# Sample values in the areas of the transposed input, the recurrence on head tiles, and an output stage that begins in halves

## The reference

```
h = rms_norm(x) @ w_in          # 8720 columns: q, k, v of 3 x 8 heads, az, gq, gk, gv, gz, glr, gates mg_a, mg_b
o_attn = softmax-weighted sum over three groups of windowed attention: (window 128, dilation 1), (512, 4), (2048, 16)
         sample tokens attend to cached k, v rows and to their own new rows
o_gla  = gated linear recurrence, 4 heads, key 64, value 128, state S:
         o = (q e^b)(k e^-b)^T masked @ v + (q e^b) @ S ;  S' = e^b_last * S + (k e^(b_last-b))^T @ v
mixed  = sigmoid(mg_a) * ((o_attn * silu(az)) @ w_attn_out) + sigmoid(mg_b) * ((rms_norm(o_gla) * silu(gz)) @ w_gla_out)
y      = rms_norm(x + mixed @ w_out)
```

## Time and profile before

| | |
|---|---|
| Median of three runs | 2516.12 us |
| The profiled execution, its own time | 2519.2 us |
| Its span, first to last instruction | 2517.4 us |
| TensorE busy | 2462.3 us, 98% of the span |
| VectorE, ScalarE, GpSimd busy | 1216.4, 907.9, 197.1 us |
| DMA moved | 416.97 MB, mean 166 GB/s |
| Chain that ended last | TensorE 93%, DMA 3%, VectorE 2% |
| Mean granted TensorE clock | 0.992 of full |

### The profile page before, as it was taken

One profiled execution on the slowest core, in us unless ns is written; L12 is line 12 of the kernel. 1 busy time (PEld: TensorE's weight loads), 2 busy tenths in 40 slices (PEclk: granted clock), 3 DMA queues, 4 the chain that ended last, 5 costly groups with the idle time before them and its releaser, 6 DMA issues.

```text
span 2517.4 us, 36888 instructions
## 1 busy us (share of the span) xinstructions
PE 2462.3 (98%) x13660; PEld 1976.9 (79%) x13660; DVE 1216.4 (48%) x2858; ACT 907.9 (36%) x2161; POOL 197.1 (8%) x360
## 2 busy tenths in 40 slices
PE   9999999999999999999999999999999977999998
PEld 6888887887778888887888888787777634888887
DVE  5323423243321125565665666557665346655663
ACT  5224534443432224224545544555243322212221
POOL 0000000000000000121111111222222100000000
PEclk9999999999999999999999999999999988999999
DMA  5333333232333224467777656887776598343431
GB/s 191 103 121 112 104 110 116 89 99 91 119 106 99 90 78 141 141 193 232 219 220 222 208 180 208 258 255 229 209 223 206 193 322 314 149 159 139 160 153 67
DMA packets 204929, 416.97 MB, mean 166 GB/s; under 512 B 32160, under 2 KB 46000, under 8 KB 202640
## 3 DMA queue, kind: packets, MB, share of 16 engines
q1 hardware_dynamic: 163360, 295.69, 35.3%
q0 software_dynamic: 29072, 92.96, 12.8%
q10 hardware_dynamic: 12320, 25.96, 2.7%
HBM read 313.33 MB, written 112.99 MB: 169 GB/s over the span
## 4 chain that ended last, share of the span: by engine, by line
PE 93%; DMA 3%; DVE 2%; SPq 1%; ACT 1%; issue 1%; POOL 0%; DVEq 0%; ACTq 0%
PE b_acc L1229 20%; PE b_acc L1231 19%; PE b_acc L1230 19%; PE c_p_s L1279 3%; PE c_p_o L1302 3%; PE c_p_t L1290 3%; PE c_p_qk L1266 3%; PE f_p_b L1894 2%; PE f_p_b L1896 2%; PE f_p_b L1895 2%; PE f_p_z L1894 2%; PE f_p_z L1896 2%; PE f_p_z L1895 2%; PE b_acc L1235 2%; PE b_acc L1236 1%; PE e_p_o L1824 1%
## 5 line engine op out<-in xcount | busy, mean ns | idle before, releaser
L1229 PE MATMUL b_acc<-b_whi,hT_hi 128*128 128x512 f32 x2048 | 819.5, 400 | 3.7 <-DVE b_wlo L965 1.5
L1231 PE MATMUL b_acc<-b_whi,hT_lo 128*128 128x512 f32 x2048 | 799.0, 390 | 0.0
L1230 PE MATMUL b_acc<-b_wlo,hT_hi 128*128 128x512 f32 x2048 | 798.3, 390 | 0.0
L1229 PEld LDWEIGHTS b_acc<-b_whi,hT_hi 128*128 128x128 f32 x2048 | 384.4, 188 | 100.9 <-issue 9.4
L1231 PEld LDWEIGHTS b_acc<-b_whi,hT_lo 128*128 128x128 f32 x2048 | 384.4, 188 | 82.5
L1230 PEld LDWEIGHTS b_acc<-b_wlo,hT_hi 128*128 128x128 f32 x2048 | 385.0, 188 | 73.3
L965 DVE SCALAR_TENSOR_TENSOR b_wlo<-b_raw,a_lnw,b_whi 128x512 fp32r<-128x512 f32 x268 | 192.8, 749 | 362.2 <-ACT b_whi L757 361.8
L771 ACT COPY b_stage<-b_acc 128x512 f32<-128x512 f32 (+2 forms) x198 | 115.3, 583 | 539.6 <-PE b_acc L1231 529.4
L795 ACT ACTIVATE c_sm<-c_sm,c_ends 128x256 f32<-128x256 f32 (+1 forms) x384 | 172.8, 451 | 129.7 <-DVE c_ends L1050 129.6
L757 ACT ACTIVATE b_whi<-b_raw,a_lnw 128x512 fp32r<-128x512 f32 x268 | 182.8, 714 | 3.8 <-ACT c_og L813 1.4
L769 ACT ACTIVATE b_stage<-b_acc 128x512 f32<-128x512 f32 x96 | 57.4, 598 | 308.4 <-PE b_acc L1231 308.2
(11 more groups left out here) (308 smaller groups left out, 3104.1 us busy)
## 6 DMA issues: line engine op xcount, KB each, us to landing
b_raw<-in_w_in SPq DMA_DIRECT2D x134, 512.0 KB, 4.4
tm<-b_stage SPq DMA_DIRECT2D x256, 256.0 KB, 2.1
a_x<-tm POOLq DMA_DIRECT2D x192, 256.0 KB, 5.0
b_ck<-in_cache_kv_w POOLq DMA_DIRECT2D x104, 256.0 KB, 5.2
c_qk<-tm SPq DMA_DIRECT2D x101, 256.0 KB, 3.7
f_m<-tm SPq DMA_DIRECT2D x16, 1024.0 KB, 5.8
c_v<-tm SPq DMA_DIRECT2D x53, 256.0 KB, 4.0
og<-c_og ACTq DMA_DIRECT2D x48, 264.0 KB, 4.1
```

The costliest lines, as they stand in the source:

```text
L1229: nc.tensor.matmul(out, stat_hi, mov_hi, start=(k == 0), stop=False)
L1230: nc.tensor.matmul(out, stat_hi, mov_lo, start=False, stop=False)
L1231: return nc.tensor.matmul(out, stat_lo, mov_hi, start=False, stop=(k == KC - 1))
```

## The change

- The value tiles 5 to 12 (`HV`) are loaded into the areas of `hT_hi` and `hT_lo`: token tile t of the second half gives its place to value tile 5 + t when the last slot that reads it is done. A tile lies there in four units, two in each of the two areas, a unit as four pieces of 128 columns with a stride of 1024, and is loaded by four DMAs (two for the half tile). SP issues them in the loop of the projection, in the last eight slots. Tiles 18 to 20 (`HV_AGAIN`) go to the places of tiles 5 to 7 once these are used. The rest pass through the ring of five.
- The recurrence's states are loaded without zeros, 128 x 128 a pair of heads and sequence; `gla_out` does two products of 64 rows by 128 columns where it did one of 128 x 256, `gla_outer(j)` does two sequences in eight products of 64 x 64 by 128; there are four `gla_outer` instead of eight. The clearing of the state on GpSimd goes.
- The branch weights have four raw buffers (`w_raw2` lies in the room that the smaller state leaves). All eight splits come after tile 20 has been used. SP's order of loads is written out anew.
- The output stage begins in another order: half of branch product 1, the mixed transposes of tile 0, the other half; VectorE's `mix(0)` is taken apart in `weigh` and `add`, and the output weights are split around them. The first two output weights are loaded as soon as all value tiles are used.

The diff, cut to its core:

```diff
+                    if s > NSLOT - TPH:
+                        late_tile(s - (NSLOT - TPH) - 1)
...
+HV = range(VSLOTS, VSLOTS + TPH)
+HV_AGAIN = range(18, 21)
...
+        v_h = [h_sb("e_v_hT_hi", [P, KC, HTOK]), h_sb("e_v_hT_lo", [P, KC, HTOK])]
...
-            G["state"] = sb("g_state", [P, DB, NP, 2 * GV_W])
+            E = dict(vc=[sb("e_vc_whi", [P, 4, CH])], v_h=v_h)
+            E["w_raw2"] = sb("w_raw2", [P, 2, D])
+            G["state"] = sb("g_state", [P, DB, NP, GV_W])
...
-    p_go = g_bank[1][0:NS, :]
-    p_u = [g_bank[2], g_bank[0]]
+    p_go = [g_bank[1][0:NS, 0:NP * GV_W], g_bank[2][0:NS, 0:NP * GV_W]]
+    p_u = [g_bank[k][:, :].rearrange("p (j a e) -> p j a e", j=2, a=NP) for k in (0, 2)]
...
+    in_h = lambda w: w in HV or w in HV_AGAIN
+    ring = [w for w in range(V_PER_PAIR * NPAIR) if not in_h(w)]
+    h_tile = lambda w: w - (HV_AGAIN.start if w in HV_AGAIN else HV.start)
+    h_loads = lambda w: 32 if w % V_PER_PAIR == 0 else 64
+
     def vc(w):
-        return vc_a[:, w % VSLOTS, :, :] if w % VSLOTS < 2 else vc_b[w % VSLOTS - 2]
+        k = ring.index(w) % VSLOTS
+        return vc_a[:, k, :, :] if k < 2 else vc_b[k - 2]
+
+    def v_cols(w, u):
+
+        if not in_h(w):
+            return vc(w)[:, u, :]
+        t = h_tile(w)
+        return v_h[u // 2][:, 4 * (u % 2):4 * (u % 2) + 4, t * P:(t + 1) * P]
...
+            if w in HV:
+                sp.wait_ge(over.mm_done, over.products - TPH + h_tile(w) + 1)
+            elif w in HV_AGAIN:
+                sp.wait_ge(v_used, HV[h_tile(w)] + 1)
+            elif ring.index(w) >= VSLOTS:
+                sp.wait_ge(v_used, ring[ring.index(w) - VSLOTS] + 1)
...
+            if in_h(w):
+                t = h_tile(w)
+                for u in range(2 if r == 0 else 4):
+                    sp.dma_start(v_cols(w, u), src[:, u, :].rearrange("l (x e) -> l x e", x=4)).then_inc(v_h_in[t // 4], 16)
+                return
...
-            wb_after = (6, 7, 9, 10, 14, 15, 18, 20)
-            for w in range(VSLOTS, V_PER_PAIR * NPAIR):
...
+            for k in range(STAGES):
+                sp.wait_ge(over.stored[k], over.stores[k])
+            sp.wait_ge(over.scored, over.scores)
+            load_vn(1)
+            sp.dma_start(diag[:, :], A["dec_diag"]).then_inc(gw_in, 16)
+            sp.dma_start(gw[:, :], A["gla_norm_w"].rearrange("a (p b) -> p (a b)", b=1)).then_inc(gw_in, 16)
+            sp.dma_start(g_v[:, :], TMs[SEQ:TOK, TM_GV * CH:(TM_GV + 1) * CH]).then_inc(g_st_in, 16)
+            load_v(13)
+            load_v(14)
+            for h in range(GH):
+                r = slice(GK * (h % 2), GK * (h % 2) + GK)
+                sp.dma_start(g_state[r, :, h // 2, :], A["state_gla"][0, :, h, :, :].rearrange("b k v -> k b v")
+                             ).then_inc(g_st_in, 16)
+            for w in (15, 16, 17):
                 load_v(w)
...
-            sp.wait_ge(v_used, 24)
+            for i in range(4):
+                load_wb(i)
+            for w in HV_AGAIN:
+                load_v(w)
+            load_vn(2)
+            branches_free(sp)
+            load_branches(0)
+            load_gates(0)
+            load_v(21)
+            load_vn(3)
+            sp.wait_ge(g_o_evacd, 1)
+            sp.dma_start(OL[SEQ:TOK, :], g_out[:, :]).then_inc(g_stored, 16)
+            for w in range(22, 26):
+                load_v(w)
+            load_branches(1)
+            load_wb(4)
+            load_v(26)
+            load_wb(5)
+            load_v(27)
+            load_wb(6)
+            load_wb(7)
+            sp.wait_ge(w_lo, 2 * G4)
+            load_m(0)
+            sp.wait_ge(v_used, 25)
...
+            sp.wait_ge(v_used, V_PER_PAIR * NPAIR)
+            load_wo(0)
+            load_wo(1)
             load_branches(2)
             load_gates(2)
             gla_over(sp)
             sample_over(sp)
-            wo = A["w_out"].rearrange("a (c p) e -> p (a c) e", p=P)
-            for c in range(KC):
-                if c >= 4:
-                    sp.wait_ge(w_lo, 2 * G4 + c - 3)
-                sp.dma_start(wo_raw[c % 4], wo[:, c, :]).then_inc(wo_in[c % 4], 16)
-                if c == 3:
-                    load_m(0)
+            for c in range(2, KC):
+                load_wo(c)
...
-                    nc.tensor.matmul(p_go[:, 2 * GV_W * a:2 * GV_W * (a + 1)], g_qm[:, a, NS * j:NS * j + NS],
-                                     g_state[:, j, a, :], start=(a == 0 and j == 0), stop=False)
-            for h in range(GH):
-                cols = slice(GV_W * h, GV_W * (h + 1))
-                last = nc.tensor.matmul(p_go[:, cols], g_att[:, h % 2, h // 2, :], g_v[:, cols], start=False,
-                                        stop=(h == GH - 1))
+                    for h in range(2):
+                        r = slice(GK * h, GK * h + GK)
+                        last = nc.tensor.matmul(p_go[h][:, GV_W * a:GV_W * (a + 1)], g_qm[r, a, NS * j:NS * j + NS],
+                                                g_state[r, j, a, :], start=(a == 0 and j == 0), stop=False)
+            last.then_inc(g_o_done, 1)
...
+            if j == 1:
+                pe.wait_ge(g_o_evacd, 1)
             if j >= 2:
-                pe.wait_ge(g_u_read, NP * (j - 1))
-            for a in range(NP):
-                cols = slice(2 * GV_W * a, 2 * GV_W * (a + 1))
-                last = nc.tensor.matmul(p_u[j % 2][:, cols], g_km[:, a, j, :], g_v[:, cols], start=True, stop=True)
+                pe.wait_ge(g_u_read, 2 * NP * (j - 1))
+            for i in range(2):
+                for h in range(GH):
+                    a, r = h // 2, slice(GK * (h % 2), GK * (h % 2) + GK)
+                    last = nc.tensor.matmul(p_u[j % 2][r, i, a, :], g_km[:, a, 2 * j + i, r], g_v[:, GV_W * h:GV_W * (h + 1)],
+                                            start=True, stop=True)
...
-                pe.wait_ge(w_lo, 2 * G4)
+                pe.wait_ge(w_lo, G4)
                 pe.wait_ge(outed, 2 * NPAIR - 3)
-            for a in range(2):
+            for a in parts:
                 if t == 0 and a == 1:
+                    pe.wait_ge(w_lo, 2 * G4)
...
-            gla_outer(1)
             pv_new(2)
             pv(2, 0, 0)
             pv(2, 1, 0)
+            gla_outer(1)
+            pv(2, 2, 0)
+            turn_p(3)
             gla_outer(2)
+            pv(2, 2, 1)
             gla_outer(3)
-            turn_p(3)
-            pv(2, 2, 0)
-            gla_outer(4)
-            gla_outer(5)
-            pv(2, 2, 1)
-            gla_outer(6)
-            gla_outer(7)
             pv_new(3)
             pv(3, 0, 0)
             pv(3, 1, 0)
             pv(3, 2, 0)
             transpose_branches(0)
             pv(3, 2, 1)
-            for t in range(TILES):
+            branch_products(0)
+            transpose_branches(1)
+            keep_running(12)
+            branch_products(1, (0,))
+            transpose_mixed(0)
+            branch_products(1, (1,))
+            out_products(0, 0)
+            transpose_branches(2)
+            out_products(0, CH)
+            transpose_mixed(1)
+            for t in range(2, TILES):
...
+            act.wait_ge(raw_in[i % 4], 16 * (i // 4) + 16)
+            act.wait_ge(v_used, HV_AGAIN.stop)
...
+            scale_ol(0)
+            for i in range(2 * G4):
+                split_wb_hi(i)
...
         def mix(t):
+            weigh(t)
+            add(t)
+
+        def weigh(t):
...
+            output(2)
+            for i in range(G4):
+                split_wb_lo(i)
             gla_advance(3)
-            split_wb_lo(5)
-            gla_advance(4)
-            gla_advance(5)
-            output(2)
-            gla_advance(6)
-            gla_advance(7)
-            gn_steps()
-            split_wb_lo(6)
-            split_wb_lo(7)
-            branches(0)
+            for i in range(G4, 2 * G4):
+                split_wb_lo(i)
             split_lo1(0)
             output(3)
             branches(1)
-            for c in range(4):
+            split_wo_lo(0)
+            split_wo_lo(1)
+            weigh(0)
+            split_lo1(1)
+            add(0)
+            for c in range(2, 6):
                 split_wo_lo(c)
-            for t in range(TILES):
+            split_lo2(0)
+            for c in range(6, KC):
+                split_wo_lo(c)
+            branches(2)
+            for t in range(1, TILES):
```

More of the change, by code:

```diff
@@ L1466, in plan_late @@
 def plan_late(nc):
+    over_h, h_sb, _, _ = scope(nc)
+    with over_h:
+        v_h = [h_sb("e_v_hT_hi", [P, KC, HTOK]), h_sb("e_v_hT_lo", [P, KC, HTOK])]
     held, h_sb, _, _ = scope(nc)
@@ L1571, in finish @@
     mask_in, lse_in, gw_in = sem("e_mask_in"), sem("e_lse_in"), sem("w_gw_in")
-    raw_in = [sem("w_raw_in0"), sem("w_raw_in1")]
+    v_h_in = [sem("e_v_hT_in0"), sem("e_v_hT_in1")]
+    raw_in = [sem(f"w_raw_in{k}") for k in range(4)]
     w_hi, w_lo = sem("w_hi"), sem("w_lo")
@@ L1702, in tail, with tile @@
                 load_v(q + 1)
+        def tile(t):
```

(15 more changed lines are left out.)

165 lines of the change are left out of this document (71 added, 94 removed).

## The result

The changed kernel, called after in this text, takes 2503.32 us (median of 5 runs, 2502.86 to 2504.80), the kernel before in the same comparison 2518.88 us (5 runs, 2514.57 to 2519.72): the ratio is 0.9945, 95% interval 0.9930 to 0.9959. It is 15.6 us faster. The profiled execution of after takes 2504.8 us, 14.4 less than that of before. The forecast of 2490 us promised 25.7 us between the profiled executions; 2503 lies inside the range of 2475 to 2504, but the gain is little more than half of what was forecast.

A forecast was written before the change was run, and what follows sets the result against it. The sample stage was taken as bound by the bytes behind its value tiles, with half-idle DMA engines just ahead. 2519.2 - 18.7 - 7.0 = 2493.5 us profiled; the median shown is 3.1 lower, so 2490, range 2475 to 2504.

The forecast's parts named there:

- Gain 36.8 - 29.0 - 0.8 = 7.0 us: First branch product to first output product: 29.0 us instead of 36.8, 0.8 for transposes moved later; bounds -9.4 and -3.
- new wait of 2.4 us: Output stage, ahead of the first half of branch product 1: TensorE waits 2.4 us in place of 6.6.
- The sample stage: Projection end to first branch product: early head tiles bring that product 18.7 us earlier, ends 11.1 and 26.4.
- The price of the pieces: Head tiles loaded in 512 B pieces: 270 GB/s, 3.9 us a tile, with ends 4.8 and 3.0 us.
- TensorE loses nothing to this before 1999.4: End of the projection: loading head tiles there costs TensorE 0 us, since a slot's store is wanted about 23 us later.
- both new waits: Sample stage: TensorE waits 6.1 us at the recurrence's small inputs and 6.3 us at the new values of pair 2.
- no waits for the value tiles of pairs 0 and 1: Sample stage, sign in the profile after: TensorE no longer waits for these value tiles.
- the recurrence products: Recurrence on head tiles: 64 records take 3.5 us, where 16 products took 7.07 us before.
- the first (full rate): Rival on head tile loads: 512 B pieces go at 392 GB/s like large ones, giving 2481 us; chance 0.13.
- the third (a price from 7 us a tile upwards): Rival: costly pieces make head tiles fill the queue far into the sample stage, 2533 us at 125 GB/s; chance 0.05.
- The second: Rival: small pieces go at 217 GB/s and output weights come late, gain 11.1 + 3, 2502 us; chance 0.13.
- The fourth: Rival: sample stage doesn't shrink, late splits and SP's order take back the gain, only the output part remains, 2509; chance 0.06.

The follow-up runs named there:

- the second experiment: Changed kernel with the first two output weights issued ahead of the final norm weight and the four state stores; 2503.51 us, ratio 0.9942.
- the kernel with four reorderings: Changed kernel with state stores, three small inputs and pair 2's new values issued earlier, four weight pieces behind the reloaded area tiles; 2493.51 us, ratio 0.9904.

## Why the prediction was wrong

**The step that failed** is the start of the output stage: "Gain 36.8 - 29.0 - 0.8 = 7.0 us". With the transposes behind O counted as there, it measured 2.0. Of the 5.0 us between O at X + 29.0 and at X + 34.0, the wait ahead of product 1 is 2.1 (4.5 for 2.4) and the first half of product 1 2.9 (8.4 for 5.5). After's profile is one of the longer ones here: over the four kernels with this output part untouched the shortfall is 3.1 to 5.3 us, and in each of them the wait and the slow half after it are there. The prediction had charged half clock after waits in the sample stage and counted its disappearance as a gain here, but put no half clock behind its own new wait of 2.4 us. And the wait was longer. ScalarE gets the first output weight at X + 12.3, not X + 11.3, after SP took 4.25 us to issue the state stores and 3.83 for the two weights; and from there to the end of both low parts it is 3.6 us (1.05 on ScalarE, 2.39 on VectorE), where 2.3 had been put. That VectorE's split also waits for the state stores stood in no step; in after they don't end the wait, but the second experiment shows that they do as soon as the weights are early. The experiment with the stores first shows what the step is worth when nothing is late: X to O 26.68, the 29.0 without its wait of 2.4. The working of the instructions was right, the landing behind it was not.

**The sample stage**, 18.7 us forecast, 14.4 measured. The mechanism was right, and loading under the projection carries it. In distances from S, with the forecast's first: the small inputs 11.6 and 13.9, the new values of pair 2 48.9 and 52.2, the end of the last area tile 66.6 and 69.7, X 85.2 and 89.5. The 2.3 us lost before the first wait ended are not what the stage lost: the kernel with the small inputs first takes 4.9 us off this wait, and S to X stays at 89.2. The loss of 3.3 us at the new values of pair 2 is. SP issues them from S + 47.1 on, when by the forecast the bytes ahead of them were just through, but they are in use only 5.1 us later, not 1.8:

```profile
2048.54 1.72 SPq L1698 DMA_DIRECT2D e_vn_a<-tm  x3
```

At the end of the last area tile it is still 3.1 us, and the rest of the stage loses 1.2 more. The price of the pieces is not it: 3.6 us a tile is below the 3.9 taken. The working added bytes only, and SP's list has more than bytes. The small inputs are five DMAs that SP issues one after the other from 2008.70 to 2012.15, each with its own landing, and behind them come further small ones; meanwhile the queue runs dry, as this view of 2012 to 2016 us in after shows:

```profile
DMA packets 673, 0.45 MB, mean 113 GB/s; under 512 B 420, under 2 KB 480, under 8 KB 673
q1 hardware_dynamic: 673, 0.45, 54.1%
```

At the end, X waits for the low part of branch 0, which stands on VectorE behind the last weight piece. ScalarE gets that piece 9.5 us after the issue of tile 27 (2077.73), where 8.1 were forecast. Tile 27 itself took 6.9 us from its issue to TensorE (2084.67) where an empty queue gave 5.4, and its 16 records ran at half clock (5.35 instead of 3.65 us), but this half clock costs nothing. In the kernel with 32 filling products the 16 records run at full clock, and X comes 6.1 us after their start (at 2093.14, after a wait of 2.4 us), in after 6.25. The last piece in after, and the 16 records in the kernel with 32 filling products:

```profile
2087.26 1.15 ACT L2123 ACTIVATE w_wb_hi<-w_raw,w_gw 128x1024 fp32r<-128x1024 f32 x1 [0.28 <-DMA w_raw<-in_w_gla_out]
```
```profile
2087.07 3.65 PE L1887 MATMUL e_p_o<-e_vc_a,e_pm 128*64 128x512 f32 x16 [2.76 <-DMA e_vc_a<-in_cache_kv_w]
```

**The projection.** "TensorE loses nothing to this before 1999.4" was wrong too, by little. From the product of `a_pt` that stands at 1932.28 us in before to S are 67.12 us in before and 67.12 in the kernel without early loads; in the nine profiles with them it is 67.68 to 69.45. A part is a wait for VectorE's softmax of the sample, whose mask is now issued behind head tiles and holds VectorE for 4.3 us in the kernel with four reorderings. TensorE's wait is 1.8 us there, the most of all, and is not seen in two of the nine, after among them:

```profile
1978.95 0.55 PE L1859 MATMUL e_bank<-ident,sT 128*128 128x128 f32 x3 [1.79 <-DVE e_wd L2321]
```

In after this loss is 0.6 of the 2.0 us; the other 1.4 stood already at 1932 us, ahead of all changed code, and are drift between executions.

**What held:** both new waits at their places, no waits for the value tiles of pairs 0 and 1, the recurrence products, the price of the pieces between its ends. Of the rivals, the first (full rate) and the third (a price from 7 us a tile upwards) are excluded by 290 GB/s. The second named late output weights and took 3 us for that term; this half of it is what happened, though not its price of a tile. The fourth said that late splits and SP's order take back what the bytes gave; SP's order took back part of the gain, but the stage did shrink, by 14.4 us. The forecast kernel was in reach: reordering SP's list gives 2491 us, at the forecast 2490, but by a shorter output part (10.2 us instead of 7.8) and S to X 82.4 instead of 85.2.

**Left open:** why X to O differs by 2.2 us between kernels with the same output part, what the early loads cost TensorE in the projection beyond the named wait, and why the new values of pair 2 show no releaser. The pieces' rate was seen only for these strides; tiles laid so that they arrive in 2 KB pieces were not tried.

## What to carry to other kernels

When loads move into an idle half of the queue, the bytes come out near what was worked out, and what remains is SP's list: work it out as issue times and landings, not as bytes alone, and ask for each small transfer which wait it ends. A split or mix that waits for a semaphore waits for all of its conditions; before moving a load forward, look for the store or the other engine that the same instruction waits for, here the state stores in `gla_over`. Behind a new wait of TensorE put the half clock as a cost of its own (2.8 us after the wait ahead of product 1), unless another engine sets what comes next, as ahead of X; and where nothing else helps, fill the wait. Before a distance of one profile against another is called a gain, look at how it scatters between kernels that don't differ there.

## What the runs showed of the hardware

- Pieces of 512 B written to 128 partitions of SBUF: 290 GB/s alone in the queue at full share, against 383 to 392 for large ones (a factor of 1.3).
- The time that SP needs to issue a DMA varies: in after two DMAs of 0.5 MB in all took between 1.05 us (at 2006.08) and 5.82 us (at 2033.22, behind large loads), and the small DMAs behind them shifted by this.
- The granted clock after a wait of 4.5 us was 0.64 over the next 8.4 us; with filling products up to 0.98 us before, it was 1.00, and the same records took 5.6 us.
- The same projection ended up to 6.7 us apart between executions (S at 1998.8 to 2005.5 in the nine profiles with early loads), so a stage's gain has to be read from distances within one execution. These scattered by 3.1 us over the 90 us from S to X and by 2.2 us over the 34 from X to O, between kernels that don't differ there.
